# State-space stage: the D·x term moved from diagonal matmuls to GpSimd, and the turns of the mixed rows moved one chunk later

## The reference, cut to what matters

```python
def ssm_mixer(z, xbc, dt_f_raw, dt_b_raw, conv_w, conv_b, dt_bias, a_log, d_skip, g_out, init_f, init_b):
    ...
    y_f, fin_f = ssd_chunked(xs, dt_f, a_f, bm, cm, init_f)
    y_b, fin_b = ssd_chunked(flip(xs), flip(dt_b), a_b, flip(bm), flip(cm), init_b)
    y = y_f + flip(y_b) + d_skip.astype(f32)[:, None] * xs.astype(f32)
    y = y.reshape(b, l, SSM_WIDTH) * jax.nn.silu(z.astype(f32))
    return rms_norm(y, g_out).astype(z.dtype), fin_f, fin_b
```

## Time and profile before

| what | value |
|---|---|
| median, lowest, highest of three runs | 1677.48, 1676.98, 1681.02 us |
| span of the profiled execution (first to last instruction) | 1673.4 us |
| time outside the span, against the median | 4.1 us |
| busy, share of the span | PE 97%, PEld 86%, DVE 58%, ACT 42%, POOL 6% |
| the chunk loop in the profile | 356 to 430 us |

### The profile page before, as it was taken

One profiled execution on the slowest core, in us unless ns is written; L12 is line 12 of the kernel. 1 busy time (PEld: TensorE's weight loads), 2 busy tenths in 40 slices (PEclk: granted clock), 3 DMA queues, 4 the chain that ended last, 5 costly groups with the idle time before them and its releaser, 6 DMA issues. The chain is left out here.

```text
span 1673.4 us, 25918 instructions
## 1 busy us (share of the span) xinstructions
PE 1623.2 (97%) x10275; PEld 1439.5 (86%) x10275; DVE 975.2 (58%) x1549; ACT 699.8 (42%) x1268; POOL 101.4 (6%) x123
## 2 busy tenths in 40 slices
PE   5999999999899999999999999999999999999997
PEld 4787878877688989878889999999999999888886
DVE  4653644268755555554687555554554555477788
ACT  4632112357554544545663333333333333434453
POOL 1101000013000000320000000000000000000011
PEclk9999999999999999999999999999999999999999
DMA  9323441013200000323312222222222226763355
GB/s 371 148 98 144 166 146 52 1 53 106 75 20 1 14 1 2 107 89 134 129 56 83 93 90 81 106 78 94 90 98 72 100 81 211 229 225 95 121 169 190
DMA packets 76295, 176.41 MB, mean 105 GB/s; under 512 B 10352, under 2 KB 26944, under 8 KB 74128
## 3 DMA queue, kind: packets, MB, share of 16 engines
q1 hardware_dynamic: 72080, 169.75, 29.1%
q0 software_dynamic: 4096, 5.01, 0.9%
HBM read 131.02 MB, written 43.70 MB: 104 GB/s over the span
## 5 line engine op out<-in xcount | busy, mean ns | idle before, releaser
L373 PE MATMUL psF<-gv,gu_ring 128*128 128x320 f32 x1224 | 378.6, 309 | 3.8 <-DVE gv L2712 3.1
L375 PE MATMUL psF<-gv,gu_ring 128*128 128x320 f32 x1224 | 378.2, 309 | 0.0
L374 PE MATMUL psF<-gv,gu_ring 128*128 128x320 f32 x1224 | 378.2, 309 | 0.0
L373 PEld LDWEIGHTS psF<-gv,gu_ring 128*128 128x128 f32 x1224 | 229.7, 188 | 4.7 <-issue 3.6
L374 PEld LDWEIGHTS psF<-gv,gu_ring 128*128 128x128 f32 x1224 | 229.7, 188 | 0.0
L375 PEld LDWEIGHTS psF<-gv,gu_ring 128*128 128x128 f32 x1224 | 229.7, 188 | 0.0
L373 PE MATMUL psF<-d_w_ring,d_hid_ring 128*128 128x512 f32 x360 | 140.2, 389 | 0.0
L374 PE MATMUL psF<-d_w_ring,d_hid_ring 128*128 128x512 f32 x360 | 140.1, 389 | 0.0
L375 PE MATMUL psF<-d_w_ring,d_hid_ring 128*128 128x512 f32 x360 | 140.0, 389 | 0.0
L373 PE MATMUL psP<-hT_hi,win_hi 128*128 128x512 f32 (+1 forms) x336 | 123.6, 368 | 1.8 <-DVEq L1078 1.5
L375 PE MATMUL psP<-hT_hi,win_lo 128*128 128x512 f32 (+1 forms) x336 | 119.2, 355 | 0.0
(11 more groups left out here) (442 smaller groups left out, 3393.5 us busy)
## 6 DMA issues: line engine op xcount, KB each, us to landing
hid_variants<-hraw SPq DMA_DIRECT2D x77, 320.0 KB, 2.2
d_hid<-hid_variants SPq DMA_DIRECT2D x58, 320.0 KB, 3.0
m_wring<-in_w_mod SPq DMA_DIRECT2D x16, 1024.0 KB, 4.8
d_b<-in_w_down SPq DMA_DIRECT2D x44, 256.0 KB, 3.7
win_raw<-in_w_in SPq DMA_DIRECT2D x18, 512.0 KB, 5.7
w_mod_staged<-in_w_mod SPq DMA_DIRECT2D x16, 512.0 KB, 14.9
d_hid_more<-hid_variants SPq DMA_DIRECT2D x19, 320.0 KB, 3.0
raw_gu<-in_w_gate SPq DMA_DIRECT2D x11, 512.0 KB, 4.3
```

What stands on the lines that cost most here:

```text
L373: pe.matmul(out, w_hi, x_hi, start=first, stop=False, skip_group_check=onto)
L374: pe.matmul(out, w_hi, x_lo, start=False, stop=False, skip_group_check=onto)
L375: return pe.matmul(out, w_lo, x_hi, start=False, stop=last, skip_group_check=onto)
```

## The change

D·x is no longer made by TensorE. GpSimd makes it for each chunk during the sweep, as soon as `xs(c)` is there (one product of 128 x 512, into the place of `xbcT` that the turn has read), from a `d_skip` that one small transfer spreads over the partitions. In the chunk loop GpSimd then adds D·x to the backward part (line 707) and the result to the forward part (line 709), and VectorE waits for that (`y_summed`) ahead of line 1164's addition. VectorE's own sum (1157), the diagonal matmuls (1433) and the `ddiag` constants go. The turn of chunk c-2 now stands on TensorE ahead of the decays of chunk c+1, and on ScalarE `mix(c - 2)` comes first in the iteration and `scale(c - 1)` last, behind `weigh(c + 1)`.

```diff
@@ -667,6 +668,7 @@ GpSimd
             p.link(pool.memset(nh[:], -0.5))
+            pool.dma_start(dskip, L.dram["d_skip"].to_broadcast([P, SH])).then_inc(d_loaded, 16)
@@ -693,9 +695,23 @@
+            pool.wait_ge(d_loaded, 16)
+            for i, c in enumerate(down):
+                pool.wait_ge(x_copied, 2 * i + 1)
+                p.mark(pool.tensor_tensor(heads4(xd(c)), heads4(xs(c)), per_head(dskip), ALU.mult))
+            p.wait()
+
+            def carried(c):
+
+                pool.wait_ge(off_b_read, c + 1)
+                p.link(pool.tensor_tensor(quads(off_b[:]), quads(off_b[:]), xd(c), ALU.add))
+                pool.wait_ge(off_f_read, c + 1)
+                pool.tensor_tensor(yv[:, c % 2, :], yv[:, c % 2, :], off_b[:], ALU.add).then_inc(y_summed, 1)
+
             pool.wait_ge(s_ready, NS)
             for c in range(NT):
                 decay(c)
+                carried(c)
                 if c >= 1:
                     rstd(c - 1)
@@ -837,9 +853,6 @@ ScalarE
-                elif i == 6:
-                    for a in range(4):
-                        act.activation(ddiag[:, a, :], L.ident, ACT.Copy, scale=dskip[:, a:a + 1]).then_inc(consts, 1)
@@ -885,15 +898,16 @@
             for c in range(NT):
+                if c >= 2:
+                    mix(c - 2)
                 if c >= 1:
                     square(c - 1)
                 if c + 1 < NT:
                     exponents(c + 1)
+                    weigh(c + 1)
                 if c >= 1:
                     scale(c - 1)
-                    mix(c - 1)
-                if c + 1 < NT:
-                    weigh(c + 1)
+            mix(NT - 2)
@@ -1152,14 +1166,11 @@ VectorE
-                dve.wait_ge(off_f_read, c + 1)
-                dve.wait_ge(off_b_read, c + 1)
-                f.link(dve.tensor_tensor(yv[:, c % 2, :], yv[:, c % 2, :], off_b[:], ALU.add))
-
                 if c + 1 < NT:
                     next_state(c)
                     weights_in_chunk(c + 1)
 
+                dve.wait_ge(y_summed, c + 1)
                 dve.wait_ge(diag_done, c + 1)
@@ -1421,6 +1432,11 @@ TensorE
                 mm.then_inc(off_done, 1)
+                if c >= 2:
+                    pe.wait_ge(cb_read, c + 1)
+                    if c >= 3:
+                        pe.wait_ge(mix_ready, c - 2)
+                    y_turn(c - 2)
                 if c + 1 < NT:
                     segments(c + 1)
@@ -1429,21 +1445,15 @@
-                for a in range(4):
-                    pe.matmul(A[3][:, chunk(a)], L.xbcT[:, a, chunk(c)], ddiag[:, a, :], start=(a == 0), stop=False)
...
-                if c >= 1:
-                    if c + 1 < NT:
-                        pe.wait_ge(cb_read, c + 2)
-                    if c >= 2:
-                        pe.wait_ge(mix_ready, c - 1)
-                    y_turn(c - 1)
+            pe.wait_ge(mix_ready, NT - 2)
+            y_turn(NT - 2)
```

More of the change, by code:

```diff
@@ L68 @@
 MOD_ALL = 6 * D // MOD_W
-C_GPRE, C_GFFN, C_BMOD, C_GQ, C_GKV, C_CW, C_CB, C_GS, C_DB, C_AL, C_DS = 0, 8, 16, 64, 67, 69, 93, 101, 105, 121, 137
-N_COLS = 141
+C_GPRE, C_GFFN, C_BMOD, C_GQ, C_GKV, C_CW, C_CB, C_GS, C_DB, C_AL = 0, 8, 16, 64, 67, 69, 93, 101, 105, 121
+N_COLS = 137
 K_ID, K_MASK, K_SEL, K_FOLD, K_TRI, K_SA, K_SB, K_MT, K_MD, K_SUM, K_SUM4 = 0, 128, 384, 400, 528, 656, 672, 672, 688, 704, 706
@@ L424, in phase_front @@
         maskb = at("maskb", "conv_acc", 0, [P, 2, 4, P], BF16)
-        ddiag = at("ddiag", "conv_acc", 2048, [P, 4, P])
+        dskip = at("d_skip", "conv_acc", 2048, [P, SH])[:]
         identb = at("identb", "conv_acc", 4096, [P, P], BF16)
@@ L478, in phase_front @@
         L.q_in, L.kv_in = ([L.own_sem(f"at_{n}_in{b}") for b in range(3)] for n in ("q", "kv"))
+        d_loaded = L.own_sem("ss_d_loaded")
         L.mix_stored, L.fin_out = mix_stored, fin_out
@@ L481, in phase_front @@
          s_ready, cb_done, cb_read, seg_done, exp_done, off_done, off_f_read, off_b_read, w_ready, diag_done, y_ready, squared,
-         rstd_ready, yn_ready, y_turned, mix_ready, sf_ready, dec_ready, fin_mm, fin_cp, consts, pch) = (
+         rstd_ready, yn_ready, y_turned, mix_ready, sf_ready, dec_ready, fin_mm, fin_cp, consts, pch, y_summed) = (
              L.sem("ss_" + n) for n in (
@@ L486, in phase_front @@
                  "off_f_read", "off_b_read", "w_ready", "diag_done", "y_ready", "squared", "rstd", "yn_ready", "y_turned", "mix_ready",
-                 "sf_ready", "dec_ready", "fin_mm", "fin_cp", "consts", "pch"))
+                 "sf_ready", "dec_ready", "fin_mm", "fin_cp", "consts", "pch", "y_summed"))
         block = st.enter_context(nc.Block())
@@ L535, in phase_front @@
         per_head = lambda ap: ap.rearrange("p (a r) -> p a r", r=2).unsqueeze(3).to_broadcast([P, 4, 2, SP_])
-        dskip = L.cols[:, C_DS:C_DS + 4]
+        xd = lambda c: L.xbcT[:, 0:4, chunk(c)]
         up2 = L.up2
@@ L1391, in y_turn @@
                 mm.then_inc(y_turned, 1)
-            pe.wait_ge(consts, 9)
+            pe.wait_ge(consts, 5)
             pe.wait_ge(ones_set, 1)
@@ L1438, in _ @@
                         mm = pe.matmul(A[3][rows, h * SP_:(h + 1) * SP_], wt[:, c % 2, h, rows],
-                                       xs(c)[:, h // 2, (h % 2) * SP_:(h % 2 + 1) * SP_], start=False, stop=(h == SH - 1))
+                                       xs(c)[:, h // 2, (h % 2) * SP_:(h % 2 + 1) * SP_], start=(h == 0), stop=(h == SH - 1))
                 mm.then_inc(diag_done, 1)
-                if c >= 1:
-                    if c + 1 < NT:
-                        pe.wait_ge(cb_read, c + 2)
-                    if c >= 2:
-                        pe.wait_ge(mix_ready, c - 1)
-                    y_turn(c - 1)
+            pe.wait_ge(mix_ready, NT - 2)
+            y_turn(NT - 2)
             pe.wait_ge(off_f_read, NT)
@@ L3333 @@
             col(a["g_ssm_out"][0]), np.tile(a["dt_bias"].reshape(1, 16), (P, 1)),
-            np.tile(a["a_log"].reshape(1, 16), (P, 1)),
-            np.repeat(a["d_skip"][0].reshape(4, 2).T, P // 2, axis=0)], axis=1),
-        "b_mod": a["b_mod"], "g_post_mix": a["g_post_mix"], "g_post_ffn": a["g_post_ffn"],
+            np.tile(a["a_log"].reshape(1, 16), (P, 1))], axis=1),
+        "d_skip": a["d_skip"], "b_mod": a["b_mod"], "g_post_mix": a["g_post_mix"], "g_post_ffn": a["g_post_ffn"],
         "w_mod": w_mod.reshape(KD, P, MOD_ALL, MOD_W).transpose(2, 1, 0, 3).reshape(MOD_ALL, P, KD * MOD_W), "w_in": np.stack([k_tiles(in_tile(*e)) for e in TILES] + z_tiles),
```

## The result

The changed kernel takes 1699.07 us (median of four runs, 1696.14 to 1702.25) against 1677.23 us for the kernel before: ratio 1.0126, 95% interval 1.0111 to 1.0142. It is slower by 21.8 us. The forecast was 1689.5 with a range of 1682 to 1695: the sign was right, the size about half of what came, and the result lies above the range. The profiled execution of the changed kernel took 1696.14 us with a span of 1694.3, 20.9 longer than before.

A forecast was written before the change was run, and what follows sets the result against it. TensorE bounds the kernel before at 7.39 us a chunk; after the change GpSimd's circle does, 15.95 + 1.3 per pair. Loop +9.5 and end +2.5 give +12.0 on a span of 1673.4, plus 4.1 outside: 1689.5, range 1682 to 1695.

The forecast's parts named there:

- Which circle sets the pace: Chunk loop: the circle of waits through GpSimd, 15.95 us per two chunks, makes pick late and TensorE wait at the decays.
- ScalarE's circle: Chunk loop: new one-chunk circle of waits, decays through exponential, weightings and scaling to the turn, 7.59 us against 7.39 before.
- The collision: Chunk loop: GpSimd's small root operations held beside VectorE's 1130 and 1133, 1.3 us per two chunks, bounds 0 to 1.9.
- The first long distance: Loop start: chunk 0 at 356.08, additions held 1.10 us by 1130 and 1133, chunk 2 at 372.4, chunk 3 at 380.0.
- The end: Loop end: last scaling 4.98 us behind line 1151 instead of 2.52, +2.5; from there to the last mix unchanged, 5.2.
- the clock at nothing: Chunk loop: the forecast charged 0 us for a lower TensorE clock, with idle pieces of 1.3 to 4 us a chunk.
- case D: Rival, chunk loop: worse, by a fallen clock (one chunk's 6.4 us taking up to 12.8) or late landings; 1697 us, chance 0.07.
- Rival A: Chunk loop: GpSimd's additions run undisturbed, 15.95 us per pair of chunks; +7.0, 1684.5 us, chance 0.19.
- B: Rival, chunk loop: pick is not late and ScalarE's circle sets the pace at 7.59 us; +4.1, 1681.6 us, chance 0.10.
- C: Rival, chunk loop: TensorE keeps the pace with less work, 6.40 us a chunk; -6.1, 1671.4 us, chance 0.04.

## Why the prediction was half right

*Which circle sets the pace*: right. Two additions of 1.28 stand ahead of root and pick, TensorE stands in even chunks for pick, and the short distances are 7.61, near the 7.59 of ScalarE's circle; with the clock held TensorE waits there 0.64 us for the scaling. But the decays that are late are those made in even chunks, of chunks 3, 5, 7 and 9 (chunk 2's aside, 1.23 us late at 362.44); my sum had those of the even ones. Two idle additions gave 18.0 us where the changed kernel lost 21.8, falls of the clock included in both.

*The collision*: right in kind, at its upper bound. The 1.85 us instead of 1.3 were made up by pick, whose first product follows the issue by 2.55 us (370.46 to 373.01) where I took 3.15.

*The first long distance*: short by 1.0. I let chunk 3 follow chunk 2 by 7.6 and had it at 380.0, 23.9 behind chunk 0; with the clock held it comes 24.9 behind. The pair of the long and the short distance begins one chunk earlier than I had it. I followed the first pick, for chunk 2, and had it held up to 361.3; it was issued at 359.87, since the second addition came first and line 1144 was the one held (2.33). The second pick, for chunk 3, I didn't follow: it stands behind the first root and was the late one (370.46).

*The end*: the scaling at 4.91 for 4.98; "From there to the last mix at 430.02 the chain is the same 5.2 us" failed, it is 7.35 at the lower clock.

*ScalarE's circle as a cost of the late turn*: not there. It gives 7.59 by the terms, and late turn alone ran at 7.46, TensorE being busy throughout, with no change in time.

*The step that failed* is the clock at nothing. The prediction gave case D 0.07, and argued that "The idle pieces between 352 and 430, where the granted clock stayed 1.00, speak against it." These were 3.9 us in 78, none over 1.1 but where the loop begins. My own sum made pieces of 1.3 to 4 us a chunk, with a lower clock seen behind one of about 4, and I still went by the case that had no such pieces. The runs: 6.2 us of the loop (82.77 less 76.62 with TensorE kept busy), some 2 at the end, 8.7 in the median. With the clock held the change costs 13.1 (1690.33 less 1677.24) where I had 12.0; 13.1 and 8.7 are the 21.8. The rule that I quoted and then set aside (the Trainium skill, "TensorE: Matmul & The Clock Gate", section "What's actually happening": the throttled state is the default, activity releases it) is borne out: with activity put in, and nothing taken out, the clock stayed up and the time came down.

Rival A (no collision) falls by the rows of the root; B and C by pick's waits. The price I gave D, 1697 by one fall of up to 6.4 us, was near for another reason: it was three smaller falls in the loop, 1.6 to 2.6 us each, and one at its end.

## What to carry to other kernels

An engine with 26 us of work in 78 isn't free: what counts is what is queued behind the new work on it, here a transfer that TensorE needs two chunks later. Move such issues ahead of the work before adding to it. And when a sum gives the bounding TensorE new waits, price the clock together with them: here three pairs of waits, 2.75 to 3.25 us each, cost another 1.6 to 2.6 in the work behind them. A gain in one stage ends at the queue that guards the next; look there for what comes back.

## What the runs showed of the hardware

The clock doesn't answer to the length of a wait alone. In the changed kernel it fell at 371.5, right behind a wait of 2.61 us; at 392.0, in the second of two waits of 2.02 and 1.09; and at 412.5, behind 1.63 and 1.12. In the same trace it stayed up behind 1.75 and 1.08 (429.19 and 430.90), with pick first behind 2.39, and with the old turn behind single waits of 3.53, 3.50 and 3.50 us (383.36, 427.81 and 437.87, where the turn took its 0.63). What decides between the two stays open: I have no run that places single waits of known length. The same kernel takes different times by it: over 29 runs of the kernel before on one chip the time goes from 1674.41 at a mean clock of 0.997 to 1681.77 at 0.993, and over the 29 the two go together (correlation -0.95). Most of the spread of this kernel goes with the clock, and single runs that differ by 0.3% say nothing.

A float32 product of a 128x128 tile was executed as two of 0.12 us: twenty of them took 4.70.

A GpSimd operation on one element per partition takes 0.19 us alone and 1.04 beside a VectorE addition of two tiles of 128x1024: small as it is, it is held for 0.85 us.
